# Second block's attention: dilated scores issued a unit ahead, the softmax division moved into the transposes, stick-breaking tables by pairs of heads, and the output projection waiting tile by tile

## The reference, cut to what matters

```python
xn = rmsnorm_2(x, attn_norm_g[l])
proj = xn @ w_in[l]
y_pool = pool_mixer(u_pool, pool_w[l], pool_scale[l])
y_dil = dilated_attention(qkv_dil, rel_bias)
y_sb = stick_breaking_attention(qkv_sb)
y_s5 = s5_mixer(u_s5, ...)
for bi, yb in enumerate((y_pool, y_dil, y_sb, y_s5)):
    gate = jax.nn.sigmoid(xn @ w_gate[l, bi])
    merged = merged + gate * (yb @ w_branch[l, row:row + width])
x = x + merged @ w_out[l]
```

```python
s = jnp.where(mask, s + bias, -1e30)
m = jnp.max(s, axis=-1, keepdims=True)
p = jnp.exp(s - m)
den = jnp.sum(p, axis=-1, keepdims=True)
o = jnp.einsum('bdhnqk,bdhnke->bdhnqe', p, vb) / den
```

## Time and profile before

| what | value |
|---|---|
| median of 3 runs | 2010.64 us (2010.11 to 2015.3) |
| profiled execution | 2010.08 us, its span 2008.3 us |
| mean granted clock of TensorE over the span | 0.937 of full speed |
| PE busy | 1758.7 us, 88% of the span |
| DVE, ACT, POOL busy | 441.8, 283.2, 116.0 us |
| second block, from its first projection to the end | 1333.9 to 2008.3 us |
| the part that the change touches | 1399 to 1717 us, and the start of `x2` |

### The profile page before, as it was taken

The page is one execution under the profiler, slowest core; times in us unless marked ns, Lnnn a source line. Parts: engine busy times, 40 slices in busy tenths (PEclk is TensorE's granted clock), DMA queues, the critical chain, the costliest instruction groups (busy, mean ns, idle before and its releaser), DMA issues.

```text
span 2008.3 us, 20729 instructions
## 1 busy us (share of the span) xinstructions
PE 1758.7 (88%) x8412; PEld 1055.8 (53%) x8412; DVE 441.8 (22%) x995; ACT 283.2 (14%) x571; POOL 116.0 (6%) x259
## 2 busy tenths in 40 slices
PE   7999999697997788969689778769998999899997
PEld 4535674143343324414235332357776878688885
DVE  2235221011111111201111110132466522211101
ACT  4023221011011100101101010011322200100000
POOL 1000000000000000004660000000011000000000
PEclk9999999797999898979899988879998999999998
DMA  9226356999999999899999999923434225244340
GB/s 380 99 86 231 144 206 237 420 419 414 417 416 374 419 413 414 364 419 417 416 417 417 407 419 414 378 75 114 163 131 142 88 101 189 103 170 168 112 161 21
DMA packets 135845, 547.01 MB, mean 272 GB/s; under 512 B 10109, under 2 KB 23549, under 8 KB 99774
## 3 DMA queue, kind: packets, MB, share of 16 engines
q1 hardware_dynamic: 129200, 529.83, 66.4%
q0 software_dynamic: 3200, 11.01, 1.5%
q10 hardware_dynamic: 3342, 4.77, 0.6%
HBM read 537.97 MB, written 7.60 MB: 272 GB/s over the span
## 4 chain that ended last, share of the span: by engine, by line
PE 74%; DMA 15%; SPq 4%; DVE 3%; ACT 2%; issue 1%; ACTq 0%; DVEq 0%
PE PS L1126 15%; DMA ring<-in_w 8%; PE PS L1142 7%; DMA arena<-in_w 6%; PE PS L1924 4%; PE PS L2080 4%; PE PS L2090 4%; PE PS L2082 4%; SPq L1590 4%; PE PS L1945 3%; PE PS L1096 3%; PE PS L1937 3%; PE PS L1122 3%; PE PS L1154 2%; PE PS L497 2%; PE PS L582 1%
## 5 line engine op out<-in xcount | busy, mean ns | idle before, releaser
L1126 PE MATMUL PS<-ring,arena 128*32 128x512 f32 (+2 forms) x1288 | 326.5, 670 | 64.8 <-DMA arena<-in_w 34.2
L1126 PE MATMUL PS<-arena 128*32 128x512 f32 (+2 forms) x760 | 214.4, 665 | 25.6 <-DMA ring<-in_w 21.0
L1126 PEld LDWEIGHTS PS<-ring,arena 128*32 128x32 f32 (+2 forms) x1288 | 103.0, 141 | 243.3 <-issue 243.3
L1142 PE MATMUL PS<-ring,arena 128*32 128x512 f32 (+2 forms) x584 | 152.3, 741 | 36.5 <-DMA ring<-in_w 23.7
L1142 PE MATMUL PS<-arena 128*32 128x512 f32 (+2 forms) x440 | 133.9, 710 | 37.8 <-DMA ring<-in_w 23.1
L1410 DVE TENSOR_SCALAR arena<-PS 128x512 f32<-128x512 f32 x28 | 19.2, 687 | 548.9 <-PE PS L1126 548.9
L1126 PEld LDWEIGHTS PS<-arena 128*32 128x32 f32 (+2 forms) x760 | 65.7, 141 | 122.5 <-issue 122.4
L1142 PEld LDWEIGHTS PS<-ring,arena 128*32 128x32 f32 (+2 forms) x584 | 44.7, 149 | 116.6 <-issue 115.6
L1924 PE MATMUL PS<-arena,ring 128*128 128x256 f32 x448 | 100.4, 385 | 5.7 <-DVE arena L2219 5.7
L1142 PEld LDWEIGHTS PS<-arena 128*32 128x32 f32 (+2 forms) x440 | 41.5, 153 | 110.3 <-issue 110.3
L1924 PEld LDWEIGHTS PS<-arena,ring 128*128 128x128 f32 x448 | 85.8, 193 | 18.9 <-DVE arena L2219 6.1
(11 more groups left out here) (408 smaller groups left out, 2030.0 us busy)
## 6 DMA issues: line engine op xcount, KB each, us to landing
ring<-in_w SPq DMA_DIRECT2D x234, 1024.0 KB, 18.7
arena<-in_w SPq DMA_DIRECT2D x150, 1024.0 KB, 18.8
ring<-in_w_ada SPq DMA_DIRECT2D x24, 1024.0 KB, 7.5
ring<-in_w_in SPq DMA_DIRECT2D x22, 1024.0 KB, 11.0
ring<-in_w_up SPq DMA_DIRECT2D x20, 1024.0 KB, 9.6
ring<-in_w_gate SPq DMA_DIRECT2D x16, 1024.0 KB, 6.6
ring<-in_w_down SPq DMA_DIRECT2D x11, 1024.0 KB, 7.4
ring<-in_w_out SPq DMA_DIRECT2D x8, 1024.0 KB, 5.0
```

Source lines behind the costliest of these rows:

```text
L1126: m = pe.matmul(bank(("up", i, b))[rows[n], :], xs[:, k, rows[n]], tiles[n][:, b * 512:(b + 1) * 512], start=False, stop=k == 7, skip_grou ...
L1142: m = pe.matmul(bank(("down", i, c))[rows[n], :], actT[:, k, rows[n]], tiles[n][:, a:a + 512], start=k == 0, stop=k == 7, skip_group_check ...
```

## The change

Four edits, and one that goes with them.

1. `attention_steps` issues a unit's scores (part 0) before the preceding unit's parts 1 and 2. Before, the two units of an hs went together: both parts 0, both parts 1, both parts 2.
2. Division: the probabilities stay undivided. In part 1, DVE takes the reciprocal of the sums and scales the identity's rows by it into `dil_d`, a diagonal of 128 by 128; PE multiplies each block by this diagonal where it was transposed against the identity. The negation goes into the maximum. What was one DVE stretch in part 0 is now two, the second of them in part 1.
3. Stick-breaking: Exp and Ln are taken for the two heads of a pair together, after both have had Copy and Abs.
4. `x2` waits for each tile of `mg` ahead of the product that reads it, where it waited for all.
5. `put(rec)` follows every third filler (n % 3 == 1), where it was every fourth (n % 4 == 2).

```diff
@@ attention_steps
-            first = [("bias_of", 0)]
-            for hs in range(4):
-                if hs < 3:
-                    first.append(("bias_of", hs + 1))
-                for i in range(3):
-                    for t in range(2):
-                        yield first + [("dil", hs, t, i)]
-                        first = []
+            units = [(hs, t) for hs in range(4) for t in range(2)]
+            for n in range(len(units) + 1):
+                if n < len(units):
+                    hs, t = units[n]
+                    first = [("bias_of", 0)] if n == 0 else []
+                    if t == 0 and hs < 3:
+                        first.append(("bias_of", hs + 1))
+                    yield first + [("dil", hs, t, 0)]
+                if n:
+                    yield [("dil",) + units[n - 1] + (1,)]
+                    yield [("dil",) + units[n - 1] + (2,)]
@@ the fillers' loop
-            if n % 4 == 2:
+            if n % 3 == 1:
                 put(rec)
@@ tensor_post, dil part 1
-                                i = pe.transpose(psum(s + (a,), b * 128, (b + 1) * 128), x[:, (a + b) * 128:(a + b + 1) * 128], ident)
+                                i = pe.matmul(psum(s + (a,), b * 128, (b + 1) * 128), x[:, (a + b) * 128:(a + b + 1) * 128], dil_d[DILS.index((hs, t)) % 2], start=True, stop=True, skip_group_check=True)
@@ tensor_post, x2
-                    w.wait_ge(mg_ready, plan.ups["mg"])
                     room(G[s])
                     for k in range(8):
+                        w.wait_ge(mg_ready, T["mg", (3, k)])
@@ scalar_post, stick part 0
                         own.count(act.activation(e_, z, ACT.Abs))
-                        own.wait()
-                        own.count(act.activation(e_, e_, ACT.Exp, scale=-1.0))
-                        own.wait()
-                        act.activation(e_, e_, ACT.Ln, bias=1.0).then_inc(stick_z, 1)
+                        if h % 2:
+                            pair = [wide[wide_of["stick", n] % 2][:, 384:768] for n in (h - 1, h)]
+                            own.wait()
+                            for v in pair:
+                                own.count(act.activation(v, v, ACT.Exp, scale=-1.0))
+                            own.wait()
+                            for v in pair:
+                                act.activation(v, v, ACT.Ln, bias=1.0).then_inc(stick_z, 1)
@@ vector_post, dil
-                        own.count(dve.tensor_reduce(dmx[n], xx, AX_X, ALU.max))
-                        own.wait()
-                        dve.tensor_scalar(dmx[n], dmx[n], -1.0, None, ALU.mult).then_inc(dil_max, 1)
+                        dve.tensor_reduce(dmx[n], xx, AX_X, ALU.max, negate=True).then_inc(dil_max, 1)
+                    elif i_ == 1:
                         w.wait_ge(dil_exp, n + 1)
                         own.count(dve.reciprocal(dden[n], dden[n]))
+                        if n >= 2:
+                            old = DILS[n - 2]
+                            w.wait_ge(pe_done, G[("dil",) + old + (1, 3 * old[1])].n)
                         own.wait()
-                        dve.tensor_scalar(xx, xx, dden[n], None, ALU.mult).then_inc(dil_p, 1)
+                        dve.tensor_scalar(dil_d[n % 2], ident, dden[n], None, ALU.mult).then_inc(dil_p, 1)
```

More of the change, by code:

```diff
@@ L1623, in build @@
         gs = [take(256) for _ in range(3)]
+        dil_d = [take(128) for _ in range(2)]
         gst = [ring[:, (6 + i) * SLOT:(7 + i) * SLOT].rearrange("p (k t) -> p k t", k=8) for i in range(2)]
```

## The result

The changed kernel takes 2043.6 us (median of 4 runs, 2043.4 to 2045.1) against 2010.5 us: the ratio is 1.0161, 95% interval 1.0146 to 1.0176. It is slower by 33 us, where 26 were forecast, and lies 0.6 us above the upper end of the stated range of 2026 to 2043. The profiled execution has a span of 2043.3 us.

The account below looks back on a forecast made before the run. PE, busy 88%, was taken to bound the kernel, its waits ended by DVE's order. Waits +16.8, products +4.0 and clock +4.8 gave +25.6 us on 2010.1: 2035.7, said as 2036 (chance 0.72), 8 in 10 range 2026 to 2043.

Parts of the forecast that it names:

- Turnings (0,0), (1,0), (1,1): PE's former transposes in dilated attention: waits of 6.0, 6.0, 5.6 us for diagonals that stand behind an `s5body` on DVE.
- Turning (0,1): Former transposes of dilated unit (0,1): PE waits 2.2 us for the diagonal behind an `s5body` of 11.7 us; no clock loss.
- poolprod: After two products PE waits 11.3 us for a bank that DVE empties behind the last `s5body`; it was 9.7.
- Three diagonals behind a branch multiplication: Turnings (2,0), (2,1), (3,0): diagonal behind DVE's multiplication of a branch tile, wait of 1.3 us each, +3.9 us.
- Stick-breaking, scores and x2: Waits at L1991 (-2.6 us, some 0.4 stays), at the scores of L2013 (-0.6) and at `x2` (-1.4) go.
- Products: Full products replace transposes for 36 blocks on PE: 0.22 us a block instead of 0.11, +4.0 us.
- The clock: PE's slower clock behind long waits: 9.2 us lost where it was 4.4, difference +4.8 us, bounds +3.6 to +7.8.
- The skill's factor of four: Transposes four times faster than float32 products; by it the products term would be 11.9 us. The prediction took two.
- The recurrence ends in time: Rival, faster: PE never waits for an `s5body`, all waits but 0.4 us go, 1992 us; chance 0.03.
- Waits overlap: Rival, no change: turnings wait only where PE waits already, so `poolprod` gives back their cost, 2010 us; chance 0.05.
- Half as slow: Rival: DVE starts `s5body` on its first inputs; three longer turning waits 3 us each, no clock cost, 2021 us; chance 0.12.
- The turning is dear: Rival, slower still: weight loads set a block's pace, 2042 us, or a product takes four transposes, 2044; chance 0.08.

Follow-up runs that it names:

- e2: The changed kernel with division back on DVE in part 0 and transposes against the identity; order and cadence as changed: 2025.3 us.
- e5: The changed kernel with `poolmix` (GpSimd's pooling sums) moved behind the transfer for `s5body 3 0`, away from `s5body 2 0`: 2039.1 us.
- e4: The kernel before with only the stick-breaking pairs and the tile by tile wait of `x2`: 2005.7 us, ratio 0.9976.
- e3: The kernel before with full products against a diagonal, made where DVE divided before; its order and cadence kept: 2011.4 us, ratio 1.0006.
- e8_placed: e6_gates_first with the copy of a dilated unit's product on ACT, recurrence pieces at chosen fillers, `poolmix` between `s5body 2 1` and `3 0`: 1991.1 us.
- e1: The changed kernel with the recurrence's pieces after every fourth filler again (n % 4 == 2), all else as changed: 2030.9 us.
- e6_gates_first: The kernel before with stick-breaking pairs, tile-wise `x2`, branch 1 gates before `poolprod`, `s5body` every third filler behind scores, `poolmix` later: 2002.6 us.

## Why the prediction was right, and where its sizes were off

The likeliest case came: slower, and by the mechanism that was named, DVE's order behind the recurrence. The time is 7.6 us over the forecast. Of the stage's 32.4 us, point by point:

- *Turnings (0,0), (1,0), (1,1)*: forecast 6.0, 6.0, 5.6 us; 5.64, 5.64 and 5.46. The working by rows held within 0.4 us each. But the prediction had only half of what holds a turning: the diagonal's place on DVE. e2 shows a second cause that was not in it, the PSUM banks that the next unit's scores fill. With the diagonal gone, the banks alone keep 15.9 of the 22.6 us at the four turnings.
- *Turning (0,1)*: forecast 2.2 us, 5.83 measured. This is the first mis-sized term, and the failing step is "an `s5body` occupies DVE for 11.7 us": it took 15.5 us beside `poolmix`. The prediction priced `s5body` from a piece that ran alone and never asked what GpSimd does beside it in the new order. e5 shows it: without `poolmix` beside it the wait is 2.0 us.
- *poolprod*: forecast 11.3 us, 11.29 measured.
- *Three diagonals behind a branch multiplication*: forecast 1.3 us each; 1.32, 1.32, 1.33.
- *Stick-breaking, scores and x2*: the 5.0 us are gone from PE's waits, where 0.4 was to stay; e4 shows -4.6 us in the stage for L1991 and `x2`. The 0.6 us at the scores went by the cadence and not by the pairs: the end was right there by luck.
- *Products*: +4.0 us; 0.22 us a block as forecast. In e3 a part was hidden where turnings stand inside a wait, which they do not here.
- *The clock*: forecast +4.8 us, and this is the second mis-sized term. Turning and filler behind the five waits took 10.7, 7.7, 6.2, 7.4 and 9.0 us; the same work undisturbed takes 7.6, 4.9, 4.1 and 4.9 us in e3 and, for two `poolprod` products and a branch tile, 6.0 us. That is 13.4 us, not the 9.2 forecast: one more long wait than thought, and 2.0 to 3.1 us behind waits of 5.5 to 5.8 us where 2.2 was taken. Before, it was 4.6 us, so +8.8, which is above the prediction's own upper bound of +7.8. The step that failed here is "between the two sizes seen, for which I take 2.2 us each": the loss doesn't follow the length of the wait. Behind the same wait of 5.64 us it was 3.1 us at (0,0) and 2.0 us at (1,0).

Sum: waits +19.3 (forecast +16.8), products +4.0, clock +8.8 (forecast +4.8), 32.1 of the 32.4 us. PE's busy time checks the last two: +13.1 us, against 4.0 + 8.8. At (0,1) `poolmix` accounts for 3.6 us of the waits and 2.8 us of the clock, about the 6.5 us by which this sum is over the forecast's 25.6; what the other long waits lost more in clock (1.2 us) and less in waiting (1.1 us) cancels.

*The range.* Its parts don't add up as stated: -1.2 and +3.0 for the clock, 1 for the diagonals and 4 for the windows around 2036 give 2030 to 2044, not 2029 to 2043. The 2043.6 us lie just inside the one and just outside the other.

*The skill's factor of four.* The Trainium skill (TensorE: Matmul & The Clock Gate, section Terms) has transposes four times faster for float32. The trace after and e3 give two: 0.22 against 0.11 us for a block of 128 by 128. By the factor of four the change would have cost 8 us more in products, and PE's busy time has no room for them.

*The rivals.* "The recurrence ends in time" needed DVE under 5.8 us for an `s5body`: it took 11.7 or 15.5. "Waits overlap" fell as well: each window began anew behind its own `s5body`. "Half as slow" counted on no loss of clock, and all five long waits lost it. "The turning is dear" needed 0.38 us a block or more, and a block took 0.22.

## What to carry to other kernels

An engine that is busy 22% of the time can still set the end, by its order: a small operation on which the bottleneck waits must not stand behind a long piece of work on its engine. Issuing work ahead helps only if neither its release nor its buffers are freed by an operation behind such a piece; price the piece beside what the other engines will then be doing. Where TensorE waited 5.5 us or more here, its clock took 2.0 to 3.1 us on top. The one kernel of these in which the pieces were placed by such rules, e8_placed, is 1.0% faster than before.

## What the runs showed of the hardware

- GpSimd and VectorE were slower beside each other: beside `poolmix` a DVE operation of 128x512 took 2.38 us instead of 0.69 and one of 128x128 1.44 us instead of 0.29, while GpSimd's first one took 2.35 us, and 1.90 us in the kernel before, where DVE was mostly idle beside it. It isn't always mutual: in e5_poolmix, GpSimd's first operation took its 1.90 us while the diagonal took 1.44 us.
- The clock behind a wait: at 2.35 us (e1) the filler behind took its usual 3.6 us; at 2.51 us (e3) it took 5.33 us, start to start, 1.8 us more. In e6_gates_first 2.74 us ahead were followed by a filler of 6.08 us, start to start. These are single waits in single executions, not a rule; why the clock falls behind one and stays behind the other was not tried.

The two rows, of e1 and of e3 (the latter's filler begins at 1612.65, the next group at 1617.98):

```profile
1496.57 1.60 PE L2023 MATMUL PS<-arena 128*128 128x128 f32 x12 [2.35 <-DVE arena L2318]
1498.01 3.62 PE L1941 MATMUL PS<-arena,ring 128*128 128x256 f32 x16
```

```profile
1617.98 0.87 PE L2034 MATMUL PS<-arena 128*64 128x128 f32 x6
```
